# Forming the running sums of the later modulation products on GpSimd, with a scale and an add, in place of one VectorE instruction

## The reference

```python
silu_c = jax.nn.silu(c)                                  # (1, 2048)
for i in range(2):
    mod_lat = silu_c @ ada_w[i] + ada_b[i]               # 2048 x 12288 weights per layer
    sh1, sc1, g1, sh2, sc2, g2 = jnp.split(mod_lat, 6)   # six vectors of 2048
    h = modulate(rms_norm(x, norm_mix_g[i]), sh1, sc1)   # h * (1 + scale) + shift
    o = latent_attention(...) @ w_o   if i == 0 else   fourier_mix(h, w_o)
    x = x + g1 * o
    x = x + g2 * sq_relu_mlp(modulate(rms_norm(x, norm_mlp_g[i]), sh2, sc2), w1, w2)
return rms_norm(x, final_norm_g)
```

## Time and profile before

| what | value |
|---|---|
| median of two runs | 2294.33 us (2291.78 and 2296.88) |
| profiled execution | 2298.68 us |
| its span (first to last instruction) | 2296.7 us |
| TensorE matmuls busy | 2121.6 us (92%) |
| VectorE busy | 1522.2 us (66%) |
| ScalarE busy | 1039.0 us (45%) |
| GpSimd busy | 84.9 us (4%) |
| mean granted TensorE clock | 0.956 |

### The profile page before, as it was taken

One profiled execution on the slowest core, in us unless ns is written; L12 is line 12 of the kernel. 1 busy time (PEld: TensorE's weight loads), 2 busy tenths in 40 slices (PEclk: granted clock), 3 DMA queues, 4 the chain that ended last, 5 costly groups with the idle time before them and its releaser, 6 DMA issues.

```text
span 2296.7 us, 25833 instructions
## 1 busy us (share of the span) xinstructions
PE 2121.6 (92%) x10675; PEld 1769.7 (77%) x10675; DVE 1522.2 (66%) x1418; ACT 1039.0 (45%) x1239; POOL 84.9 (4%) x165
## 2 busy tenths in 40 slices
PE   5989877679989999999999998998999999999997
PEld 3779676347778888887888876877888888888886
DVE  5868787786887687765666655687656644555555
ACT  4854332443354445444444444435545454444443
POOL 0001000000100000000000000000000000000000
PEclk9989987799989999999999998999999999999999
DMA  9957665245969798975767661595777655555553
GB/s 359 343 204 277 233 223 202 92 131 212 375 230 336 263 344 295 341 264 214 255 242 256 240 234 51 191 375 183 253 249 252 218 178 171 200 187 199 205 198 110
DMA packets 128017, 538.87 MB, mean 235 GB/s; under 512 B 8422, under 2 KB 9240, under 8 KB 82200
## 3 DMA queue, kind: packets, MB, share of 16 engines
q1 hardware_dynamic: 101760, 360.73, 44.3%
q0 software_dynamic: 23040, 167.78, 20.3%
q10 hardware_dynamic: 3100, 8.71, 1.0%
HBM read 535.09 MB, written 2.10 MB: 234 GB/s over the span
## 4 chain that ended last, share of the span: by engine, by line
PE 77%; DVE 13%; ACT 4%; DMA 3%; issue 3%; ACTq 0%; DVEq 0%
PE ps L1097 21%; PE ps L1053 12%; PE ps L1056 12%; PE ps L1057 12%; PE ps L1099 10%; DVE ada_sum L643 3%; DVE w_lo L628 3%; DVE hrms L782 2%; PE ps L1018 2%; PE ps L1019 2%; PE ps L1020 2%; ACT w_hi L320 1%; DMA raw<-in_ada_w 1%; DMA ada_raw<-in_ada_w 1%; PE ps L1038 1%
## 5 line engine op out<-in xcount | busy, mean ns | idle before, releaser
L628 DVE TENSOR_TENSOR w_lo<-raw,w_hi 128x1024 fp32r<-128x1024 f32 x688 | 837.0, 1223 | 618.1 <-ACT w_hi L320 617.9
L320 ACT ACTIVATE w_hi<-raw 128x1024 fp32r<-128x1024 f32 x688 | 725.3, 1059 | 992.7 <-PE ps L1057 480.4
L1097 PE MATMUL ps<-hh,w_hi 128*128 128x512 f32 x2048 | 722.4, 398 | 2.3 <-ACT g_row L406 1.4
L1099 PE MATMUL ps<-hh,w_lo 128*128 128x256 f32 x2048 | 572.8, 280 | 0.0
L1053 PE MATMUL ps<-w_hi,hh 128*128 128x512 f32 x1280 | 503.6, 393 | 16.1 <-DVE w_lo L628 10.0
L1056 PE MATMUL ps<-w_lo,hh 128*128 128x512 f32 x1280 | 502.3, 392 | 0.0
L1057 PE MATMUL ps<-w_hi,hh 128*128 128x512 f32 x1280 | 501.8, 392 | 0.0
L1097 PEld LDWEIGHTS ps<-hh,w_hi 128*128 128x128 f32 x2048 | 386.8, 189 | 97.1 <-ACT g_row L406 3.0
L1099 PEld LDWEIGHTS ps<-hh,w_lo 128*128 128x128 f32 x2048 | 387.9, 189 | 0.0
L643 DVE SCALAR_TENSOR_TENSOR ada_sum<-ada_raw,silu,ada_sum 128x2048 f32<-128x2048 f32 x150 | 351.9, 2346 | 7.2 <-DMA ada_raw<-in_ada_w 6.4
L1053 PEld LDWEIGHTS ps<-w_hi,hh 128*128 128x128 f32 x1280 | 242.9, 190 | 69.8 <-issue 13.4
(11 more groups left out here) (156 smaller groups left out, 1536.5 us busy)
## 6 DMA issues: line engine op xcount, KB each, us to landing
raw<-in_mlp_w SPq DMA_DIRECT2D x256, 1024.0 KB, 5.1
ada_raw<-in_ada_w POOLq DMA_DIRECT2D x160, 1024.0 KB, 5.3
raw<-in_ada_w SPq DMA_DIRECT2D x32, 1024.0 KB, 4.9
raw<-in_attn_w_qkv SPq DMA_DIRECT2D x24, 1024.0 KB, 6.3
raw<-in_attn_w_o SPq DMA_DIRECT2D x16, 1024.0 KB, 6.2
raw<-in_fourier_w_o SPq DMA_DIRECT2D x16, 1024.0 KB, 5.6
x_tm<-in_x ACTq DMA_DIRECT2D x1, 2048.0 KB, 15.6
c_rows<-in_ctx ACTq DMA_DIRECT2D x1, 2048.0 KB, 20.7
```

Source lines behind the costliest of these rows:

```text
L320: act.activation(w_hi[:, s % SPLIT, :], raw[:, piece % RAW, s % 2, :], ACT.Copy).then_inc(hi_ready, 1)
L628: nc.vector.tensor_tensor(w_lo[:, s % SPLIT, :], raw[:, s // 2 % RAW, s % 2, :], w_hi[:, s % SPLIT, :].bitcast(F32), ALU.subtract).then_in ...
L1097: mm(ps[:, bank, :].rearrange("p (a t) -> p a t", a=2), w_hi[:, s % SPLIT, w], hh[:, k, :, :], start=(k == 0), stop=False, skip_group_chec ...
L1099: ins = mm(ps[:, bank, 0:T], w_lo[:, s % SPLIT, w], h_hi[:, k, :], start=False, stop=(k == KT - 1), skip_group_check=True)
```

## The change

The 160 steps move from VectorE's program to GpSimd's. Where VectorE did multiply and add in one instruction, GpSimd scales the loaded block in place and then adds it to `ada_sum`, with a semaphore wait in between (`ada_scaled`). Step 0 of a vector is one instruction, the scaling straight into `ada_sum`. In GpSimd's queue load n stands in front of step n - 1. Steps are no longer tied to slices: GpSimd runs through them as fast as its waits let it. These are the block's landing, the step before, the turn of the vector before (now for the column turns too), and, for the first step, all 64 slices of the start. The bias additions and the taking of the turned vectors stay on VectorE.

```diff
+    ada_scaled = sem("ada_scaled")
...
         nc.gpsimd.memset(tick[:, 0:2], 0.0).then_inc(ticked, 1)
-        for i, (lay, m) in enumerate(SUMS):
-            for t in range(KT):
-                load_ada(16 * i + t, ada_v[lay][m, t])
+        def ada_step(v, t):
+
+            n = KT * v + t
+            pool.wait_ge(ada_in[n % 2], 16 * (n // 2 + 1))
+            if t == 0 and v - 1 in ROWS:
+                pool.wait_ge(row_T, 4 * ROWS[v - 1] + 4)
+            if t == 0 and v - 1 in COLS:
+                pool.wait_ge(col_T, COLS[v - 1] + 1)
+            if n > 0:
+                pool.wait_ge(ada_used, n)
+            else:
+                pool.wait_ge(slice_done, 2 * START)
+            col = silu[:, t, 0:1]
+            if t == 0:
+                ins = nc.gpsimd.tensor_scalar(ada_sum[:, :], ada_raw[:, n % 2, :], col, None, ALU.mult)
+            else:
+                nc.gpsimd.tensor_scalar(ada_raw[:, n % 2, :], ada_raw[:, n % 2, :], col, None, ALU.mult).then_inc(ada_scaled, 1)
+                pool.wait_ge(ada_scaled, n - n // KT)
+                ins = nc.gpsimd.tensor_tensor(ada_sum[:, :], ada_raw[:, n % 2, :], ada_sum[:, :], ALU.add)
+            ins.then_inc(ada_used, 1)
+
+        order = [(lay, m, t) for lay, m in SUMS for t in range(KT)]
+        for n, (lay, m, t) in enumerate(order):
+            load_ada(n, ada_v[lay][m, t])
+            if n >= 1:
+                ada_step((n - 1) // KT, (n - 1) % KT)
+        ada_step(9, KT - 1)
...
-        def ada_step(v, t):
-
-            n = KT * v + t
-            dve.wait_ge(ada_in[n % 2], 16 * (n // 2 + 1))
-            if t == 0 and v - 1 in ROWS:
-                dve.wait_ge(row_T, 4 * ROWS[v - 1] + 4)
-            if n > 0:
-                dve.wait_ge(ada_used, n)
-            col = silu[:, t, 0:1]
-            if t == 0:
-                ins = nc.vector.tensor_scalar(ada_sum[:, :], ada_raw[:, n % 2, :], col, None, ALU.mult)
-            else:
-                ins = nc.vector.scalar_tensor_tensor(ada_sum[:, :], ada_raw[:, n % 2, :], col, ada_sum[:, :],
-                                                     ALU.mult, ALU.add)
-            ins.then_inc(ada_used, 1)
...
-        split_block(2 * P_KV, kv_hook, kv_ada)
+        split_block(2 * P_KV, kv_hook)
...
-            split_block(2 * P_Q + 16 * b, head_hook(4 * b, 5 if b == 0 else 1),
-                        lambda p: ada_step(1, 8 * b + p))
+            split_block(2 * P_Q + 16 * b, head_hook(4 * b, 5 if b == 0 else 1))
...
         for n in range(37):
-            if n < 32 and n % 2 == 0:
-                ada_step(2, n // 2)
...
             for s in range(28):
-                if s % 2 == 0:
-                    ada_step(v, s // 2)
                 split_lo(first + s + LOOKAHEAD)
-            ada_step(v, 14)
-            ada_step(v, 15)
...
-                if s in sums:
-                    ada_step(*sums[s])
-                    if sums[s][0] in ROWS and sums[s][1] == KT - 1:
-                        add_bias(sums[s][0], g_row)
+                if s in sums and sums[s][0] in ROWS and sums[s][1] == KT - 1:
+                    add_bias(sums[s][0], g_row)
...
-                if l == 0 and s % 7 == 2 and s // 7 < KT:
-                    ada_step(7, s // 7)
-                    if s // 7 == KT - 1:
-                        add_bias(7, late_row)
+                if l == 0 and s == 7 * KT:
+                    add_bias(7, late_row)
```

More of the change, by code:

```diff
@@ L763, in kv_hook @@
                 lower_both(p + 1)
-        def kv_ada(p):
-            for t in (2 * p, 2 * p + 1):
-                ada_step(0, t)
-        split_block(2 * P_KV, kv_hook, kv_ada)
+        split_block(2 * P_KV, kv_hook)
         dve.wait_ge(slice_done, 2 * P_Q)
```

## The result

The changed kernel took 2997.85 us, median of two runs (2997.4 and 2998.3), against 2294.33 us before: a ratio of 1.307, 95% interval 1.300 to 1.313. Slower was right. The time was not: 2650 us was forecast with a range up to 2890. The profiled span is 2995.4 us.

What follows compares the result with a forecast made beforehand. TensorE, busy 92% of the span, was taken to bound the kernel, with VectorE's steps on the path only in some stretches. Late vectors summed to 353 us on 2298.7, giving 2652, stated as 2650 us, range 2310 to 2890.

Steps and rivals of the forecast that it cites:

- the shared path: Between VectorE and GpSimd: two-input or fast one-input VectorE instructions cannot run beside a GpSimd instruction; my case, chance 0.50.
- the price of the scaling: On GpSimd: one scaling of 128 x 2048 takes one unhurried pass, 2.3 us.
- the upper bound of 13.4 us: For GpSimd's instructions: the slowest rate of any row, the reciprocal's 3347 ns for 512 elements, taken to 2048.
- the sum of both engines' use: For each vector: 106 + 13 us for GpSimd plus VectorE's two-input work up to its turn.
- rival 1: Strict turns or slower instructions: VectorE gets one instruction between two of GpSimd's, 2880 us in all; chance 0.22.
- vectors 2, 7 and 9 at zero: Attention's vector at 143 us for 144, and the two with deadlines of over 300 us: no loss.
- turn 4 at 41: Vector 4, 42 w_lo and 8 remainders included, takes 175 us where it was 135: +41 us.
- the splits run up to four slices ahead: Ahead of TensorE, 8 us of work at 2.7 us a slice covers a wait of 4.6 us.
- the later one blocks fully: When a two-SBUF-input VectorE instruction meets a GpSimd instruction reading SBUF, the later waits entirely; cited from a skill page.

Runs made afterwards that it cites:

- Experiments 1: Changed kernel with GpSimd's work left in, but TensorE's turns and the bias additions read fixed tiles and wait for no vector: 2746.4 us, ratio 1.195.
- 2: Changed kernel with each GpSimd scaling and addition replaced by three memsets of the same tile, reading nothing from SBUF: 2884.8 us, ratio 1.255.
- experiment 13: Changed kernel with every GpSimd scaling and addition split into two of 128 x 1024, turns still waiting for the vectors: 2911.3 us, ratio 1.268.
- Experiment 5: Changed kernel with GpSimd's scaling by the constant 0.5 in place of the column of silu: 3043.3 us, ratio 1.326.
- experiment 9: Kernel before the change with only vector 2, attention's, on GpSimd and the other nine on VectorE: 2352.0 us, ratio 1.023.
- Experiments 6: Changed kernel with GpSimd's scaling as a tensor_tensor multiplication by the repeated column, same result computed: 3016.4 us, ratio 1.314.
- 7: Changed kernel without the scaling, so that a step is one addition on GpSimd: 2700.5 us, ratio 1.176.
- 11: Kernel before with only vectors 7 and 9 on GpSimd, scaling as multiplication by the repeated column, every instruction split in two: 2391.3 us, ratio 1.041.
- Experiment 12: Kernel before with only vectors 7 and 9 on GpSimd, instructions split in two, scaling as tensor_scalar: 2306.5 us, ratio 1.0045.

## Why the prediction was wrong

**Right: direction and the shared path.** VectorE with two SBUF inputs and GpSimd's reads hold each other up, and the turns wait. Experiments 1 and 2 show the one, the turns' brackets and experiment 13 the other. The addition was put at 4.6 us and took 4.5 us undisturbed and 4.75 in the mean; the Trainium skill's 4497 ns for it (GPSIMD Engine Reference, section 3) is near the least that the trace has, 4493 ns. My own way to 4.6 was luck: it counted 2.3 us for each input read, and the scaling, with one input, took longer than the addition with two.

**Wrong: the price of the scaling.** "One unhurried pass, 2.3 us" was 5.4 us undisturbed and 5.9 in the mean. That is 16 x 3.6 = 58 us more for each vector. The nearest row was taken from another engine, and the upper bound of 13.4 us for 2048 elements was in my own text; the range used only 0.5 us above the chosen value. Experiment 5 excludes the operand as the cause; why the form is slow stays open. The same multiplication as a tensor_tensor took 3.6 us.

**Wrong: the sum of both engines' use.** Each vector was sized as GpSimd's time plus all of VectorE's two-input work. GpSimd's time alone is 171 us (vector 2 in experiment 9, from 393.1 to 564.2), not 119. The vectors whose turns waited took 176 to 184 us (vector 5: 1124.2 to 1307.9), so VectorE's work added only 5 to 13 us where 41 to 51 were put. The step of 12.4 us shown above is also shorter than its parts, 5.44 + 4.5 for GpSimd and 4 x 1.22 for the w_lo, 14.8 us. The two errors nearly cancel: the vectors were forecast at 160 to 170 us and came out 13 to 20 us longer. These stretches lost 13 to 26 us beyond the forecast (63 to 88 us for 50 to 62), and that it was not more is luck. Nearly all of the blocking fell on VectorE, one or two of whose instructions passed for each of GpSimd's. In rival 1 I had written this: one instruction between two of GpSimd's. Experiments 6, 7 and 11 show that for tensor_tensor, but for a short one beside a load's issue. The changed kernel's trace has four w_lo in a step of a tensor_scalar and an addition.

**Wrong: nothing for what TensorE waits for directly.** This is the step that failed by most: vectors 2, 7 and 9 at zero, and turn 4 at 41. A stretch was charged only for the time by which its vector is late. VectorE's held instructions had no price of their own, and "the splits run up to four slices ahead" was taken to cover them. Measured were 61, 31 and 93 us, and 87 at turn 4.

- Vector 2: its sum of 143 us came out at the old 144 and was taken for no change. GpSimd finished it at 677.7, 33 us before its turn. Attention's scalings took 2466 ns for 487, 63 us more for the 32 (experiment 9 alone: 52 us in all).
- Vector 9 and turn 4: 81 us each ahead of the ninth slice of the up projection, where the norms and splits of the activations have no lead. GpSimd had finished vector 4 at 1082.4, 38 us before its turn.
- Vector 7: here the lead of the splits did count, and the pace broke it. In the down projection VectorE also has a product to make for each fourth slice, and while GpSimd worked a slice took it 3.4 us, for the 2.8 that TensorE needs in the up projection. Four slices of lead cover one wait, not a slower pace. TensorE waited 20 us for w_lo and 7 us for the activation behind it.

Experiment 12 bears this out for vectors 7 and 9: in halves, with instructions held for less time, the two cost 10 us together.

**The size in all.** The sum fell 346 us short. 185 of them are the stretches of vectors 2, 7 and 9, and 46 the one before turn 4. The rest is 20 us before turn 1, which did not wait for GpSimd either, and the stretches where turns waited. Seen from TensorE, its idle time grew by some 620 us, and it was busy 80 us longer over the same 10675 matmuls (2201.6 us for 2121.6), at a mean granted clock of 0.87 for 0.96; the sum had no term for that. Rival 1's total of 2880 was the nearest. It had the taking of turns right and the scaling short. But its 16 us for vector 2 was 61, its 80 for vector 7 was 31, and it too had no price for what stands ahead of the up projection, so its nearness is in part luck.

## What to carry to other kernels

Before moving VectorE work to GpSimd, count the instructions on either side, not only their time: where both need the shared path, VectorE gets one or two instructions for each of GpSimd's, and a producer that feeds TensorE must still make its pace. A lead of some buffers hides a wait, never a rate. Then look for the places where TensorE needs VectorE's result at once, with nothing prepared ahead, like a norm before a projection or the scalings of attention: there each held instruction is a wait of TensorE, however late the moved work is needed. Short GpSimd instructions help with both: two far vectors in halves cost 0.45% here, the same two whole 4.8%. But the form counts as well: halves with the multiplication still cost 4.1%.

## What the runs showed that I had not expected

- GpSimd's tensor_scalar on 128 x 2048 fp32 takes 5.4 us, with a column or a constant, its tensor_tensor by a repeated column 3.6 us, an addition of two tensors 4.5 us and a memset 1.82 us.
- The faster form was the worse neighbour: with the multiplication 2391 us, with the 1 us slower tensor_scalar halves 2306.5 us (experiments 11 and 12). A w_lo ended 0.65 us before a scaling's recorded end in the changed kernel, and 0.66 us in experiment 12, while behind additions it ended 1.1 us after. So "the later one blocks fully", as the prediction had it, does not hold up to the scaling's recorded end. That this form gives the path free before it ends is my reading of these rows; no run tried it by itself.
- The product of an SBUF and a PSUM tensor (1215 ns) and the reciprocal (3346 ns) ran at full speed beside GpSimd throughout.
- The granted clock was 0.76 to 0.83 from turn to turn between turn 0 and turn 6 and before turn 8, where TensorE waited at turns and ahead of projections. It was 0.97 from 2270 to 2400 us and 1.00 from there to turn 9, where TensorE had work almost without a break.
